# First attention of a hybrid decoder step: value, key, statistics and share jobs at other steps of each pair, and a second output buffer for the first head group

## The reference, cut to what matters

```python
for g, (window, dil) in enumerate(((128, 1), (512, 4), (2048, 16))):
    q = rope(rms_norm(qkv[:, :, 0, g], q_g[g]), pos)
    k = rope(rms_norm(qkv[:, :, 1, g], k_g[g]), pos)
    v = qkv[:, :, 2, g]
    o, lse = dilated_attention_prompt(q, k, v, window, dil)
    outs.append(o); lses.append(lse); rows.append(new)       # new: the last k and v, an output
wts = jax.nn.softmax(jnp.stack(lses, axis=0), axis=0)
o = jnp.einsum('gnthd,gnth->nthd', jnp.stack(outs, axis=0), wts)
return o.reshape(n, T, A_HEADS * HEAD_DIM) @ w_out, rows
```

## Time and profile before

| what | value |
|---|---|
| median of 3 runs | 2937.64 us (2934.67 to 2940.99) |
| profiled execution | 2938.89 us, its span 2937.1 us |
| first attention, TensorE | about 519 to 800 us of the span |
| TensorE busy over the span | 2698.7 us (92%) |
| VectorE, ScalarE, POOL busy | 1733.6, 980.9 and 740.7 us |
| mean granted clock of TensorE | 0.949 of full |

### The profile page before, as it was taken

One profiled execution on the slowest core, in us unless ns is written; L12 is line 12 of the kernel. 1 busy time (PEld: TensorE's weight loads), 2 busy tenths in 40 slices (PEclk: granted clock), 3 DMA queues, 4 the chain that ended last, 5 costly groups with the idle time before them and its releaser, 6 DMA issues.

```text
span 2937.1 us, 45747 instructions
## 1 busy us (share of the span) xinstructions
PE 2698.7 (92%) x17524; PEld 2627.8 (89%) x17524; DVE 1733.6 (59%) x2724; ACT 980.9 (33%) x1818; POOL 740.7 (25%) x362
## 2 busy tenths in 40 slices
PE   4999999778887999999999969698979999999997
PEld 3999999677776999999999958598979999999997
DVE  6787831555545565556555676795266555556555
ACT  3666632665303212121211245584132211112120
POOL 2111113344304222222222142173232222222220
PEclk7999999888788999999999989898999999999998
DMA  3322243434344343443444111444613545434331
GB/s 104 92 72 86 73 127 103 137 110 124 104 144 94 83 90 83 90 83 94 97 91 94 37 39 58 130 144 127 138 40 88 103 92 92 91 83 87 93 76 61
DMA packets 219857, 275.65 MB, mean 94 GB/s; under 512 B 29562, under 2 KB 191746, under 8 KB 217666
## 3 DMA queue, kind: packets, MB, share of 16 engines
q1 hardware_dynamic: 219746, 274.17, 37.4%
HBM read 237.90 MB, written 125.62 MB: 124 GB/s over the span
## 4 chain that ended last, share of the span: by engine, by line
PE 82%; DVE 7%; DMA 3%; POOL 2%; ACT 2%; issue 2%; SPq 1%; DVEq 0%; POOLq 0%; ACTq 0%
PE acc L347 23%; PE acc L349 23%; PE acc L348 23%; DVE arena L579 2%; PE aux L1971 2%; PE aux L1566 1%; PE acc L1491 1%; PE acc L1958 1%; PE acc L1534 1%; DVE arena L555 1%; POOL xl L533 1%; PE acc L1941 1%; PE aux L636 1%; PE aux L635 1%; PE acc L1525 1%
## 5 line engine op out<-in xcount | busy, mean ns | idle before, releaser
L347 PE MATMUL acc<-xh,w_hi 128*128 128x344 f32 x3504 | 1135.8, 324 | 65.6 <-DVE xl L533 37.0
L349 PE MATMUL acc<-xh,w_lo 128*128 128x344 f32 x3504 | 1126.5, 321 | 0.0
L348 PE MATMUL acc<-xl,w_hi 128*128 128x344 f32 x3504 | 1126.2, 321 | 0.0
L332 POOL TENSOR_TENSOR w_lo<-w_raw,w_hi 128x1024 fp32r<-128x1024 f32 x194 | 485.7, 2508 | 1761.9 <-ACT w_hi L322 1761.9
L347 PEld LDWEIGHTS acc<-xh,w_hi 128*128 128x128 f32 x3504 | 664.6, 190 | 85.1 <-issue 39.2
L349 PEld LDWEIGHTS acc<-xh,w_lo 128*128 128x128 f32 x3504 | 664.9, 190 | 0.0
L348 PEld LDWEIGHTS acc<-xl,w_hi 128*128 128x128 f32 x3504 | 664.8, 190 | 0.0
L852 DVE TENSOR_TENSOR hT<-hT,acc 128x1032 f32<-128x1032 f32 x184 | 226.3, 1230 | 387.8 <-PE acc L349 387.8
L322 ACT CAST w_hi<-w_raw 128x1024 fp32r<-128x1024 f32 x194 | 201.8, 1050 | 582.9 <-PE acc L349 495.4
L347 PE MATMUL acc<-f_hi,w_hi 128*128 128x344 f32 x1056 | 340.2, 322 | 11.1 <-DVE f_lo L1111 11.1
L349 PE MATMUL acc<-f_hi,w_lo 128*128 128x344 f32 x1056 | 339.5, 322 | 0.0
(11 more groups left out here) (261 smaller groups left out, 3202.5 us busy)
## 6 DMA issues: line engine op xcount, KB each, us to landing
out_a_w_sample<-in_cache_a_kv_w SPq DMA_DIRECT2D x23, 2848.0 KB
w_raw<-in_ffn_w_up SPq DMA_DIRECT2D x88, 512.0 KB, 3.8
scratch<-arena SPq DMA_DIRECT2D x46, 516.0 KB, 3.1
w_raw<-in_ffn_w_down SPq DMA_DIRECT2D x44, 512.0 KB, 3.5
w_raw<-in_a_w_in SPq DMA_DIRECT2D x36, 512.0 KB, 4.3
out_a_w_sample<-in_cache_a_kv_w SPq DMA_DIRECT2D x8, 2044.0 KB
arena<-in_cache_a_kv_w SPq DMA_DIRECT2D x24, 512.0 KB, 3.8
w_raw<-scratch SPq DMA_DIRECT2D x17, 512.0 KB, 3.9
```

Source lines behind the costliest of these rows:

```text
L332: pool.tensor_tensor(w_lo[:, slot, :], w_raw[:, slot, :], w_hi[:, slot, :].bitcast(F32), ALU.subtract).then_inc(lo_ready, 1)
L347: pe.matmul(out, whi, ahi, start=first, stop=False)
L348: pe.matmul(out, whi, alo, start=False, stop=False)
L349: return pe.matmul(out, wlo, ahi, start=False, stop=last)
```

## The change

It does the following, all in the first attention:

- the first key job of a pair moves from 10i - 7 to 10i - 5, and the two of the start from steps 2 and 0 to 3 and 1;
- value jobs of groups 1 and 2 move from `first_a` + 1 to `first_a` - 1 (steps 3 and 7 of a pair instead of 5 and 9); the loads and outputs of values follow them: a load is issued in the step of the job before it;
- the shares: VectorE r = 4 instead of 3, POOL's subtraction and ScalarE's exponential r = 5 instead of 3 (on ScalarE now ahead of the probabilities), sums r = 6 instead of 4 (on ScalarE now after the exponentials), the final product r = 7 instead of 5;
- weight jobs and weighing r = 8, 9, 10 instead of 6, 7, 8; additions r = 9 and 10 instead of 7 and 8; the split of the mixed output r = 11 instead of 9, and two more steps in all;
- weighing happens in place. Group 0's outputs go to `a_og[0]` for even pairs and to `a_mix` for odd ones; POOL adds group 0 into group 1's buffer and that into group 2's. The copy of group 0's outputs waits for the additions of the pair before the last, that of group 1 for all four of the last pair, that of group 2 for these and for the low part of the last mixed output.

The diff, cut to its core:

```diff
-        K_JOBS = ((-7, 0, 7, 1), (-2, 1, 4, 4), (2, 2, 0, 4), (4, 2, 4, 4))
+        K_JOBS = ((-5, 0, 7, 1), (-2, 1, 4, 4), (2, 2, 0, 4), (4, 2, 4, 4))
-        A_STEPS = A_UNITS + 10
+        A_STEPS = A_UNITS + 12
+        def weighed(i, g):
+            return a_mix if g == 0 and i % 2 else a_og[g]
-                    if k == (10 * i + K_JOBS[n][0] if 10 * i + K_JOBS[n][0] > 0 else (2, 0)[n])]
+                    if k == (10 * i + K_JOBS[n][0] if 10 * i + K_JOBS[n][0] > 0 else (3, 1)[n])]
+        def values_at(k):
+            return [x for x in range(A_GRP) if k == first_a(x) + (1, -1, -1)[x % NG]]
+        def after(k, steps):
+            return [i for i in range(A_PAIRS) if k == 10 * (i + 1) + steps]
...
             names += [("k", n) for n in key_jobs_at(k)]
-            i, r = divmod(k - 10, 10)
-            if 0 <= i < A_PAIRS:
-                names += [("stat", i)] if r == 1 else []
-                names += [("w", i, r - 6, half) for half in range(2)] if 6 <= r < 9 else []
+            names += [("stat", i) for i in after(k, 1)]
+            names += [("w", i, g, half) for g in range(NG) for i in after(k, 8 + g) for half in range(2)]
...
-                for x in range(1, A_GRP):
-                    if k == (first_a(x - 1) + 2 if x > 1 else -3):
+                for x in [1] if k == -3 else [y + 1 for y in values_at(k) if 0 < y < A_GRP - 1]:
...
-                for x in starting(k - 2):
+                for x in values_at(k - 1):
...
         def o_evac(eng, copy, x, half, done):
             i, g = divmod(x, NG)
-            if i:
-                wait_emptied(eng, ("w", i - 1, g, 1))
+            o = weighed(i, g)
+            if g == 0:
+                if i >= 2:
+                    eng.wait_ge(DA.mixed, 4 * (i - 2) + 2)
+            elif i:
+                eng.wait_ge(DA.mixed, 4 * i)
+                if g == 2:
+                    eng.wait_ge(DA.o_lo, 2 * i)
...
         def weigh_dve(v_, i, g):
-                if g == 0:
-                    v_.wait_ge(DA.o_lo, 2 * i)
-                v_.tensor_tensor(a_og[g][:, cols] if g else a_mix[:, cols], a_og[g][:, cols],
-                                 bank_a(("w", i, g, half)), ALU.mult).then_inc(DA.out_dve, 1)
+                v_.tensor_tensor(o, o, bank_a(("w", i, g, half)), ALU.mult).then_inc(DA.out_dve, 1)
...
         def attn_a_dve(v_, k0, k1):
-                if 0 <= i < A_PAIRS and r == 3:
+                for i in after(k, 4):
                     shares_dve(v_, i)
...
         def attn_a_act(act):
                     exps_a_act(act, k, 0)
-                if 0 <= i < A_PAIRS and r == 1:
+                for i in after(k, 1):
                     stats_act(act, i)
-                if 0 <= i < A_PAIRS and r == 4:
-                    sums_act(act, i)
+                for i in after(k, 5):
+                    shares_act(act, i)
                 if 0 <= k - 2 < A_UNITS:
                     probs_a(act, act.copy, k - 2, 0, DA.out_act)
                 if 0 <= k < A_UNITS:
                     exps_a_act(act, k, 1)
-                if 0 <= i < A_PAIRS and r == 3:
-                    shares_act(act, i)
+                for i in after(k, 6):
+                    sums_act(act, i)
                 for x in splitting(k):
                     split_a_act(act, x, "k")
                 for x in splitting(k - 1):
                     split_a_act(act, x, "q")
-                if 0 <= i < A_PAIRS and r == 9:
+                for i in after(k, 11):
                     mixed_act(act, i, 0)
                     mixed_act(act, i, 1)
+        def mix_pool(pool, i, g):
+            for half in range(2):
+                cols = slice(HALF * half, HALF * half + HALF)
+                wait_emptied(pool, ("w", i, g, half))
+                if g == 2:
+                    pool.wait_ge(DA.mixed, 4 * i + half + 1)
+                pool.tensor_tensor(a_og[g][:, cols], a_og[g][:, cols], weighed(i, g - 1)[:, cols], ALU.add) \
+                    .then_inc(DA.mixed, 1)
...
         def attn_a_pool(pool):
-                if 0 <= i < A_PAIRS and r == 3:
+                for i in after(k, 5):
                     shares_pool(pool, i)
-                if 0 <= i < A_PAIRS and r == 4:
+                for i in after(k, 6):
                     sums_pool(pool, i)
-                if 0 <= i < A_PAIRS and r == 5:
-                    weights_pool(pool, i)
                 for x in splitting(k):
                     split_a_lo(pool, x, "k")
                 for x in splitting(k - 1):
                     split_a_lo(pool, x, "q")
+                for i in after(k, 7):
+                    weights_pool(pool, i)
+                for g in (1, 2):
+                    for i in after(k, 8 + g):
+                        mix_pool(pool, i, g)
+                for i in after(k, 11):
+                    mixed_pool(pool, i)
```

More of the change, by code:

```diff
@@ L1454, in attn_a_sp @@
                         .then_inc(DA.k_out[stage], 16)
-                i, r = divmod(k - 10, 10)
-                if 0 <= i < A_PAIRS and r == 2:
+                for i in after(k, 2):
                     wait_emptied(sp, ("stat", i))
@@ L1591, in attn_a_pe @@
             for k in range(k0, k1):
-                for x in starting(k - 1):
+                for x in values_at(k):
                     value_rows_pe(pe, x)
@@ L1595, in attn_a_pe @@
                     key_rows_pe(pe, n)
-                i, r = divmod(k - 10, 10)
-                if 0 <= i < A_PAIRS and r == 1:
+                for i in after(k, 1):
                     stats_pe(pe, i)
-                if 0 <= i < A_PAIRS and 6 <= r < 9:
-                    weights_pe(pe, i, r - 6)
+                for g in range(NG):
+                    for i in after(k, 8 + g):
+                        weights_pe(pe, i, g)
                 if 38 <= k < 38 + NG:
@@ L1648, in o_evac @@
             i, g = divmod(x, NG)
-            if i:
-                wait_emptied(eng, ("w", i - 1, g, 1))
+            o = weighed(i, g)
[6 more added lines that the diff above has]
+                    eng.wait_ge(DA.o_lo, 2 * i)
             if g == 2:
-                if i:
-                    eng.wait_ge(DA.mixed, 4 * i)
-                copy(a_og[2].rearrange("p (n s) -> p s n", s=8)[:, 4 * half:4 * half + 4, :],
+                copy(o.rearrange("p (n s) -> p s n", s=8)[:, 4 * half:4 * half + 4, :],
                      aux[:, half, :].rearrange("p (s n) -> p s n", s=4)).then_inc(done, 1)
             else:
-                if i and g:
-                    eng.wait_ge(DA.mixed, 4 * i - 2)
-                copy(a_og[g][:, HALF * half:HALF * half + HALF], aux[:, half, :]).then_inc(done, 1)
+                copy(o[:, HALF * half:HALF * half + HALF], aux[:, half, :]).then_inc(done, 1)
         def probs_a(eng, copy, u, e, done):
@@ L1716, in weigh_dve @@
             for half in range(2):
-                cols = slice(HALF * half, HALF * half + HALF)
+                o = weighed(i, g)[:, HALF * half:HALF * half + HALF]
                 wait_job(v_, ("w", i, g, half))
@@ L1749, in attn_a_dve @@
                     key_rows_dve(v_, n)
-                i, r = divmod(k - 10, 10)
-                if 0 <= i < A_PAIRS and 6 <= r < 9:
-                    weigh_dve(v_, i, r - 6)
+                for g in range(NG):
+                    for i in after(k, 8 + g):
+                        weigh_dve(v_, i, g)
                 if 38 <= k < 38 + NG:
@@ L1801, in mixed_act @@
             act.wait_ge(DA.mixed, 4 * i + 2 + half + 1)
-            act.copy(xh[:, i, cols], a_mix[:, cols]).then_inc(DA.o_hi, 1)
+            act.copy(xh[:, i, cols], a_og[2][:, cols]).then_inc(DA.o_hi, 1)
         def attn_a_act(act):
@@ L1843, in attn_a_pool @@
                     split_a_lo(pool, x, "q")
-                if 0 <= i < A_PAIRS and r in (7, 8):
-                    for half in range(2):
-                        cols = slice(HALF * half, HALF * half + HALF)
-                        wait_emptied(pool, ("w", i, r - 6, half))
-                        if r == 8:
-                            pool.wait_ge(DA.mixed, 4 * i + half + 1)
-                        pool.tensor_tensor(a_mix[:, cols], a_mix[:, cols], a_og[r - 6][:, cols], ALU.add) \
-                            .then_inc(DA.mixed, 1)
-                if 0 <= i < A_PAIRS and r == 9:
-                    for half in range(2):
-                        cols = slice(HALF * half, HALF * half + HALF)
-                        pool.wait_ge(DA.o_hi, 2 * i + half + 1)
-                        pool.tensor_tensor(xl[:, i, cols], a_mix[:, cols], xh[:, i, cols].bitcast(F32),
-                                           ALU.subtract).then_inc(DA.o_lo, 1)
+                for i in after(k, 7):
+                    weights_pool(pool, i)
+                for g in (1, 2):
+                    for i in after(k, 8 + g):
+                        mix_pool(pool, i, g)
+                for i in after(k, 11):
+                    mixed_pool(pool, i)
```

21 lines of the change are left out of this document (13 added, 8 removed).

## The result

The change makes the kernel slower: median 2963.39 us of 4 runs (2959.68 to 2964.26) beside 2939.24 (2934.67 to 2940.99, with a fourth run of the kernel before), a ratio of 1.0074 with a 95% interval of [1.0061, 1.0088]. The profiled execution has a span of 2962.3 us, 25.2 more than before, and TensorE's mean granted clock is 0.943 instead of 0.949.

A forecast was written before the change was run, and what follows sets the result against it. Some 20 us of each middle pair were taken as waits (value load, statistics) or half-clock work. Terms -4.1 - 11.7 + 8.4 - 11.9 + 9.7 gave -9.6 us, 2928.0 against the median; 8-in-10 range 2915 to 2942.

The forecast's parts named there:

- the 17.8 us it had: First pair: step 17 starts at 603.3 instead of 621.13, 17.8 us less, 2.0 of it a moved weight job.
- Start and value jobs: Steps 0 to 12: load wait goes, ScalarE is late next, start costs about 1 us; -4.1 us in all.
- Shares: Steps 13 to 17: the statistics' wait shrinks to 1.6 us of TensorE; -11.7 us first pair, -11.9 second, zero third.
- my sign: Steps 14 and 15: the three or four waits reduced to one under 2.5 us if the forecast is right.
- the final weights to 17: Shares term: the final weights move to step 17; part of the -11.7 us for the first pair.
- I keep it for the moved jobs: Weight jobs: a fall of the granted clock to 0.57 costing 1.6 us, assumed to stay after the move.
- Pair start: Steps 21 to 23 and 31 to 33: output copies wait for POOL's additions and residual; +8.4 us first, +9.7 second.
- S + 5.4: Step 21: VectorE and ScalarE released 5.4 us after S, the end of ScalarE's split of step 20.
- Steps 34 to 40: Last pair: weight jobs beside the sample's row jobs in steps 38 to 40 cost 0.
- the third: Steps 21 and 22: ScalarE and VectorE stand behind POOL, TensorE idle and cold; slower, 2944 us at 17 each; chance 0.14.
- Rival 1: Pair starts cost about 3 us instead of 9 because TensorE has queued work; 2916 us; chance 0.20.
- the trace's row: From 614 to 624 TensorE fully busy at clock 1.00, then 0.57 while still busy; the rule would lower the sum 3.2 us.

The follow-up runs named there:

- The first experiment: In the changed kernel, POOL's final product of the shares moved ahead of the key split in its list: 2933.75 us, 0.9973 of the time before.
- The two experiments with the additions and the residual: In the changed kernel, POOL's additions, or separately the mixed output's residual on ScalarE and POOL, moved ahead of the splits: 2941.88 us and 2945.07 us.
- the residual ahead: In the changed kernel, the mixed output's high and low part moved ahead of the splits on ScalarE and POOL: 2945.07 us, 1.0022 of the time before.
- The doubled jobs: Changed kernel with final product, additions and residual ahead of the splits, every weight matmul issued twice: 2964.5 us, 1.0115 of the time before.
- the queues in order: Changed kernel with final product, additions and residual all ahead of the splits: 2908.25 us, 0.9875 of the time before.

## Why the prediction was wrong

Up to step 16 the working held in kind, with 12.1 of the 17.8 us it had; behind that it failed. Its dates laid on the ends of the steps (a job that moved across such an end shifts a term, not the sum), beside the measured differences (rounded):

```
                        predicted   measured
start, steps 0 to 11        -4.1       -2.7
steps 12 to 16             -13.7       -9.4
steps 17 to 23             +11.5      +20.3
steps 24 to 26             -14.9      -12.9
steps 27 to 33             +12.6      +23.6
steps 34 to 40              -1.0       +5.0
sum                         -9.6      +23.8
```

**Start and value jobs: right.** The load wait is gone, as foretold, and ScalarE is next (0.91 us, at 580.10). VectorE's 6.38 us behind the key output reappears a step later as 5.01. The start costs 2.6 us where I had 1, inside the bound of 4.

**Shares: right in mechanism, one wait missed and one date too early.** The exponential ends at 601.5 and the probabilities' copy at 602.0 (600.99 and 601.42 plus their 0.52 and 0.56), where I had 599.9 and 600.4. The shares' date does not follow from its own terms: 599.62 less the 4.7 us is 594.9, not 593.6. Measured it is 596.16, since the query load ahead of the statistics was issued only 2.9 us earlier than before (586.51 against 589.39). What I left out is VectorE's 2.78 us in step 15. The one-tile key job, now in that step, needs the staging buffer that step 12's four-tile job had filled at 583.02. SyncE issues that output behind the statistics' read-back, in its most crowded moment (twenty DMAs issued between 586.51 and 598.39). Issued at 595.07, it frees the buffer at about 600.0, 4.9 us on. So TensorE had one wait of 3.15 us there where my sign asked for one under 2.5. With the half-clock value matmuls behind it that is most of the 4.3 us missing in steps 12 to 16.

**The step that failed is "the final weights to 17", and with it "I keep it for the moved jobs".** The sum holds nothing for a wait in front of the three weight jobs: I priced them as TensorE work alone. ScalarE's part of the shares was indeed ready at 608.79, well before step 18 begins at 613.6. I did not look for the last link, a POOL operation of one microsecond, in POOL's list. For the additions I had done exactly that ("POOL's list for step 20 has the key split first"); for the final product of step 17 I had not, and that step's key split stands in front of it. Price: 5.0 us idle and 3.7 of slow clock in the first pair, 5.0 and 4.8 in the second. The 1.6 us per pair that I kept for a slow clock round the weight jobs assumed no wait in front of them. The first experiment takes 18.5 us away in just these steps, and those are most of the 19.8 by which the two stretches with the weight jobs (17 to 23, 27 to 33) exceeded the sum.

**Pair start: right, at a slightly higher price.** I had the copy at S + 5.4 and measured S + 5.45; TensorE idle "about 7.5" and measured 8.61; the second wait "4 to 5" and measured 4.53 and 3.86. The two experiments with the additions and the residual remove the two waits one by one. Steps 21 to 23 took 29.8 and 30.7 us where I had 28.8.

**Steps 34 to 40: wrong.** The term for the weight jobs there was 0, "use bank and VectorE time that step 36 gives back". Steps 34 to 37 came out 5.7 us shorter than before, but steps 38 to 40 took 27.9 us at clock 0.57, where the kernel before had 17.1 at 0.90 and the experiment with the residual ahead 19.4 at 0.91 with the same jobs. So the term missed the clock, and not engine time. My sign for this, a last pair off by more than 3 us, did appear.

Of the rivals, the third named the right side but not the cause. It wanted a cost of 13.9 us per pair start; steps 21 to 23 and 31 to 33 became 9.6 and 11.7 us longer than before (TensorE idle for 13.1 and 12.5 in them), and with the weights' wait out of the way the kernel was 0.27% faster than before. Rival 1 (cheap pair starts) needed another order in POOL's list, which the experiments then gave it.

On the clock, the prediction took the trace's row over the rule of the Trainium skill, "TensorE: Matmul & The Clock Gate", section "What's actually happening", that activity releases the throttle. The doubled jobs bear the row out: 0.71 with TensorE busy throughout. The same section of the Trainium skill puts the ramp's cost at under 1% of a typical span. This trace gives more, if all slow work is counted: cut into stretches of 1 us, TensorE was busy at the 1.2 GHz level for about 185 us of the kernel before, and at full clock that work would take at best half as long, an estimate of up to 92 us or 3.1% of the span. The 8.5 us between the slowest and fastest steps 38 to 40 alone are 0.3%, but the whole change, with the queues in order, was worth about 1%, so for a single edit the clock weighs as much as the waits.

What stays open: why steps 38 to 40 get 0.57 in one kernel and 0.91 in another, with the same instructions and no wait over 1 us in either. It may go with what TensorE did in the steps before, or it may differ between executions of one kernel: the ten runs of the residual ahead spread over 25 us, with mean clocks from 0.949 to 0.942, and each kernel was profiled once. No run here separates the two. That the small stationary operand itself lowers the clock is supported by the doubled jobs, but a matmul of the same shape with 128 partitions in its place was not tried.

## What to carry to other kernels

When work moves to other steps of a hand-written order, write out for each engine the whole list of the step it lands in, down to the smallest operation, and ask what stands in front of it and what that waits for; a 1 us product behind a 2.9 us split took back 18.5 of the 25 us that the change had gained in steps 0 to 16 and 24 to 26. Put short operations that another engine waits for ahead of long ones that wait themselves. A change that measures as slower can still hold 1%: undo the new waits before undoing the change.

## What the runs showed of the hardware

- TensorE's granted clock can fall without idle time: it was 0.71 over 29.60 us in which TensorE was busy for 29.60, around matmuls with a 16-partition stationary operand; steps 18 to 20 had 0.90 with half as many of them, and 1.00 in two of the three steps.
- The same 142 or 143 matmul rows took from 17.90 to 26.40 busy us, by the clock they met.
- From issue to landing, the twelve key outputs of four tiles took a median of 3.0 us in the kernel before and 4.6 in the changed one, the four of one tile 2.4 and 3.8. The four-tile output issued at 595.07 freed its buffer some 4.9 us later, and the one behind the earlier trace rows, issued at 528.52, was waited for until 533.64.
